# Sums of squares for the second block's query and key norms: two fp32r passes over parts made on GpSimd, two steps later, in place of one fp32 product

## The chip, the cores and the metric

The kernel runs on one core of one Trainium2 chip. The metric is the device time of one execution in microseconds, lower is better. The engines are called as the profile calls them: PE is TensorE, with PEld for its weight loads; ACT is ScalarE; DVE is VectorE; POOL is GpSimd; SP only issues transfers.

## What is computed

Two transformer blocks on 512 tokens of width 1024. The change lies in the second block, where the queries and keys of eight heads (those of the chunked attention with relative positions) are normalised by their root mean square over the 64 numbers of a head:

```
def rmsnorm_2(x, g):
    xf = x.astype(jnp.float32)
    y = xf * lax.rsqrt(jnp.mean(xf * xf, axis=-1, keepdims=True) + EPS)
    return (y * g.astype(jnp.float32)).astype(x.dtype)
...
        q_ca = rmsnorm_2(hs(q_ca, N_CA_HEADS), g_q[l])
        k_ca = rmsnorm_2(hs(k_ca, N_CA_HEADS), g_k[l])
        o_ca = chunked_relpos_attention(q_ca, k_ca, hs(v_ca, N_CA_HEADS), rel_bias[l])
```

## The kernel before

Large products are made from two parts of each operand: an upper part rounded to fp32r and a lower part, the rest. One product of 128x128 by 128x512 is then three fp32r matmuls (upper by upper, upper by lower, lower by upper), lines L2247 to L2249. ACT makes the upper part of each weight (L726), DVE subtracts it to get the lower part (L1306).

The stretch that the change touches is the loop over `steps_s` = 188 steps. It stands once in the program of each engine, and the order on an engine is the order in which the code was written. A step is three matmuls on PE, one eighth of a projection of 128 columns by 512 tokens. Steps 0 to 63 are eight such projections: for each pair of heads p = 0 to 3 the queries (`sub` 0) and the keys (`sub` 1), into PSUM banks 0 and 1. Steps 64 to 95 make the values of the other attention, and so on. Between steps stand "beats": scores (L2394), transposes (L2416) and value products (L2440, L2445) of the attention of heads whose queries and keys are ready. `PACE_S` says how many beats follow each step; none with work in it stands before step 33.

Each of the eight projections ends at a step n = 8m + 7, and is normalised by this chain (`SQUARES` lists the eight steps):

1. ACT squares the projection out of its bank into `sq` (L1128), at step n.
2. PE multiplies `sq` by `blk`, a matrix with ones in two 64x64 blocks, which sums the squares of a head and spreads the sum over its rows (L2678). This is one fp32 product of 128x128 by 128x512, after step n + 2 (`LAG_SUM`). I call it the sum product.
3. ACT takes Ln of the sum and Exp of -0.5 times that (L1098, L1100), at step n + 3 (`LAG_ROOT`).
4. DVE multiplies the bank by the result and by the gain into `qk` (L1780), at step n + 4 (`LAG_NORM`), and counts `qn` up by one. The bank is free then.

PE waits for `qn` before it writes a bank again. For the first seven projections that is at step n + 9 (step 16 waits for the first, and so on). For the last one, which ends at step 63, it is step 68, the first of the second block of values: four steps after step 64, because the values are made in groups of four steps.

POOL has little to do in this stretch. In the order of its program it issues the loads of the last of 48 tiles of the modulation weights (L2157; DVE's L1315 consumes them, and a load waits until the tile that had its place is consumed), then writes a masked corner into each of the eight bias tables once the table has arrived (L2180), with one small memset between the second and third (L2185).

## Time and profile before

| | us |
|---|---|
| median of 3 runs | 957.02 (956.65 to 957.07) |
| the profiled execution, its own time | 957.26 |
| its span, first to last instruction | 955.5 |
| PE busy | 943.3 (99%) |
| DVE busy | 690.3 (72%) |
| ACT busy | 563.2 (59%) |
| POOL busy | 93.7 (10%) |

Between the span and the execution's own time lie 1.8 us in which no instruction is recorded. The granted TensorE clock is full in every slice. In the timeline a matmul's duration overlaps with the next one's: what a matmul occupies of PE is the distance between starts. The fp32 sum product is recorded as two matmuls (x2).

### The profile page before, as it was taken

How to read it: one execution, taken by the hardware profiler on the slowest of the kernel's cores; microseconds unless marked ns; L12 is line 12 of the kernel's file. 1: busy time of each engine (PE TensorE's matmuls, PEld its weight loads, DVE VectorE, ACT ScalarE, POOL GpSimd, SP SyncE). 2: the span in 40 equal slices, each digit the busy share in tenths (PEclk: the TensorE clock that was granted, in tenths of full speed). 3: DMA queues.
4: the chain of work that ended last, by engine and by line, in shares of the span. 5: the costliest groups of instructions: out<-in, count | busy, mean ns of one | idle time of the engine just before them, and what ended most of it. 6: DMA issues, size and time to landing. Idle time of an engine off the chain costs nothing.

```text
span 955.5 us, 13280 instructions
## 1 busy us (share of the span) xinstructions
PE 943.3 (99%) x4728; PEld 787.9 (82%) x4728; DVE 690.3 (72%) x1270; ACT 563.2 (59%) x1107; POOL 93.7 (10%) x182
## 2 busy tenths in 40 slices
PE   8999999999999999999999999999999999999998
PEld 7878988878888887877788777898888888888887
DVE  6487888878788766667768896857544853673988
ACT  6448787753233257479987664556745634644562
POOL 4001101011122102100000000110000000000110
PEclk9999999999999999999999999999999999999999
DMA  8205222149788653833442423465877567486773
GB/s 305 86 24 190 68 79 88 50 158 348 279 316 281 201 134 127 310 111 98 128 173 72 127 67 122 142 175 136 204 215 177 164 195 194 119 233 193 171 186 110
DMA packets 34899, 156.57 MB, mean 164 GB/s; under 512 B 5242, under 2 KB 5498, under 8 KB 22163
## 3 DMA queue, kind: packets, MB, share of 16 engines
q1 hardware_dynamic: 21042, 103.51, 31.2%
q0 software_dynamic: 11152, 49.29, 21.0%
q10 hardware_dynamic: 2640, 2.93, 0.9%
q8 instruction: 38, 0.62, 0.3%
q14 instruction: 27, 0.21, 0.1%
HBM read 144.61 MB, written 5.27 MB: 157 GB/s over the span
## 4 chain that ended last, share of the span: by engine, by line
PE 85%; DVE 8%; ACT 3%; DMA 2%; issue 1%; ACTq 0%; POOL 0%; DVEq 0%; POOLq 0%
PE psum L2247 25%; PE psum L2248 25%; PE psum L2249 25%; PE psum L2416 3%; PE psum L2394 2%; PE psum L2445 1%; DMA raw<-in_wall 1%; PE psum L2440 1%; DVE wl L1306 1%; DVE p_sb L1506 1%; PE psum L2678 1%; DVE hl L1345 1%; DMA v_ca<-v_ca 1%; DVE ptl L1518 1%; DVE xt L1341 1%
## 5 line engine op out<-in xcount | busy, mean ns | idle before, releaser
L2247 PE MATMUL psum<-hh,wh 128*128 128x512 f32 (+2 forms) x736 | 277.7, 377 | 0.7 <-DVE hl L1345 0.6
L2249 PE MATMUL psum<-hh,wl 128*128 128x512 f32 (+2 forms) x736 | 270.1, 367 | 0.0
L2248 PE MATMUL psum<-hl,wh 128*128 128x512 f32 (+2 forms) x736 | 270.1, 367 | 0.0
L1306 DVE TENSOR_TENSOR wl<-raw,wh 128x512 fp32r<-128x512 f32 x336 | 218.8, 685 | 38.3 <-ACT wh L726 37.7
L726 ACT ACTIVATE wh<-raw 128x512 fp32r<-128x512 f32 x336 | 193.2, 621 | 70.3 <-PE psum L2249 64.0
L2247 PEld LDWEIGHTS psum<-hh,wh 128*128 128x128 f32 x736 | 138.4, 188 | 24.5 <-DVE hl L1345 1.6
L2249 PEld LDWEIGHTS psum<-hh,wl 128*128 128x128 f32 x736 | 138.3, 188 | 23.2
L2248 PEld LDWEIGHTS psum<-hl,wh 128*128 128x128 f32 x736 | 138.6, 188 | 20.4 <-issue 1.2
L2247 PE MATMUL psum<-wh,ah 128*128 128x512 f32 x192 | 76.1, 396 | 0.4 <-ACT p_sb L872 0.4
L2249 PE MATMUL psum<-wh,al 128*128 128x512 f32 x192 | 74.9, 390 | 0.0
L2248 PE MATMUL psum<-wl,ah 128*128 128x512 f32 x192 | 74.8, 389 | 0.0
L2416 PE MATMUL psum<-ident,p_sb 128*128 128x128 f32 (+1 forms) x272 | 46.4, 274 | 2.3 <-DVE ptl L1518 1.7
L1209 ACT ACTIVATE two<-psum 128x512 f32<-128x512 f32 x32 | 19.1, 597 | 49.0 <-PE psum L2249 48.9
L2247 PEld LDWEIGHTS psum<-wh,ah 128*128 128x128 f32 x192 | 36.1, 188 | 8.7 <-issue 1.0
L2416 PEld LDWEIGHTS psum<-ident,p_sb 128*128 128x128 f32 (+1 forms) x272 | 32.6, 135 | 12.3 <-issue 4.1
L860 ACT ACTIVATE p_sb<-p_sb,sm 128x528 f32<-128x528 f32 (+3 forms) x64 | 36.2, 565 | 11.1 <-DVE sm L1492 10.9
L2249 PEld LDWEIGHTS psum<-wh,al 128*128 128x128 f32 x192 | 36.0, 188 | 7.7
L2205 POOL DMA_DIRECT2D raw<-in_wall x20 | 17.4, 868 | 251.8 <-DMA raw<-in_wall 141.7
L2248 PEld LDWEIGHTS psum<-wl,ah 128*128 128x128 f32 x192 | 36.1, 188 | 6.7
L866 ACT ACTIVATE p_sb<-p_sb,sm 128x528 f32<-128x528 f32 (+3 forms) x64 | 35.8, 560 | 0.4 <-DVE sm L1497 0.2
L889 ACT ACTIVATE pth<-psum 128x128 fp32r<-128x128 f32 (+4 forms) x72 | 32.2, 447 | 5.9 <-PE psum L2416 5.3
L2249 PE MATMUL psum<-wh,s_y 128*128 128x512 f32 (+1 forms) x92 | 34.9, 380 | 0.0
(367 smaller groups left out, 1729.6 us busy)
## 6 DMA issues: line engine op xcount, KB each, us to landing
raw<-in_wall SPq DMA_DIRECT2D x79, 1024.0 KB, 5.5
raw<-in_wall POOLq DMA_DIRECT2D x20, 1024.0 KB, 8.0
wa<-in_wada POOLq DMA_DIRECT2D x24, 512.0 KB, 6.0
gt<-in_wada POOLq DMA_DIRECT2D x20, 512.0 KB, 6.9
xt<-in_xcols SPq DMA_DIRECT2D x8, 264.0 KB, 7.8
cb<-c_rows SPq DMA_DIRECT2D x8, 264.0 KB, 3.4
x<-in_x SPq DMA_DIRECT2D x4, 512.0 KB, 10.2
x_kept<-x SPq DMA_DIRECT2D x4, 512.0 KB, 2.9
```

Source lines behind the costliest of these rows:

```text
L726: e.activation(parts_at(w, c)[0], raw_of(w, c), ACT.Copy).then_inc(a["wh"], 1)
L860: e.activation(block_p(h, i), block_p(h, i), ACT.Exp, bias=nmx, scale=1.0 if h in FG else -1.0, accum_out=su).then_inc(a["exp"], 1)
L866: e.activation(block_p(h, i), block_p(h, i), ACT.Copy, scale=mx).then_inc(a["norm"], 1)
L889: e.activation(ph[0:rows, PT[j]:PT[j] + w_], bank[bk][0:rows, 0:w_], ACT.Copy).then_inc(a["turn"], 1)
L1209: e.activation(two[:, n % 2, :], bank[w1_bank(n)], ACT.Relu).then_inc(a["r"], 1)
L1306: e.tensor_tensor(lower_, raw_of(w, c), upper_.bitcast(F32), ALU.subtract).then_inc(v["wl"], 1)
L2205: e.dma_start(raw_at(i), wall[W_MLP + 8 * q + 4 + m], accum_op=ALU.add).then_inc(d[f"wa{i}"], 16)
L2247: e.matmul(out_, lh, rh, start=start, stop=False, skip_group_check=True)
L2248: e.matmul(out_, lh, rl, start=False, stop=False, skip_group_check=True)
L2249: return e.matmul(out_, ll, rh, start=False, stop=stop, skip_group_check=True)
L2394: ins = e.matmul(dst[:, size * j:size * j + size], q[:, 128 * i:128 * i + 128], k[:, size * j:size * j + size], start=k is k_up, stop=k is ...
L2416: ins = e.transpose(bank[bk][0:keys, 128 * (i - i0):128 * (i - i0) + 128], head(h)[0][:, o:o + keys], ident[:, :])
```

## The change

The sum product becomes two fp32r matmuls. `sq` is split first, on POOL: a copy rounded to fp32r, then the difference between `sq` and the copy, both into a new buffer `sq_parts`. PE multiplies each part by `blk` and adds them up in the bank. `blk` gets the type fp32r. The three lags grow by two: the sum product stands after step n + 4, Ln and Exp at n + 5, the multiplication at n + 6. There is one buffer for the parts, so POOL waits for the sum product before (`ss`). POOL's remaining masks are woven into its new loop over the steps. A semaphore of POOL, `rs1`, is renamed `norm`, and counts the new instructions as well.

```diff
-        blk = sb("blk", [128, 128])
+        blk = sb("blk", [128, 128], F32R)
...
+        parts_q = sb("sq_parts", [128, 2, SEQ], F32R, where=bq)
...
-        LAG_SUM, LAG_ROOT, LAG_NORM = 2, 3, 4
+        LAG_SUM, LAG_ROOT, LAG_NORM = 4, 5, 6
...
             e.wait_ge(v["m"], 24)
-            for h in CA:
+            def table_mask(h):
                 e.wait_ge(d[f"bt{h % 2}"], 16 * (h // 2 - 3))
                 e.memset(bt[h % 2][0:64, 448:512], NEG).then_inc(g["bt"], 1)
-                if h == 9:
+
+            def square_parts(p, sub):
+                n = 2 * p + sub
+                e.wait_ge(a["sq"], n + 1)
+                if n:
+                    e.wait_ge(t["ss"], n)
+                e.tensor_copy(sq_parts[0], sq[:, sub, :]).then_inc(g["norm"], 1)
+                e.wait_ge(g["norm"], 12 + 2 * n + 1)
+                e.tensor_tensor(sq_parts[1], sq[:, sub, :], sq_parts[0].bitcast(F32), ALU.subtract).then_inc(g["norm"], 1)
+
+            table_mask(8)
+            table_mask(9)
+            for n in range(steps_s):
+                if n in SQUARES:
+                    square_parts(*SQUARES[n])
+                if n == 31:
                     for j in range(4):
                         e.wait_ge(d[f"x{4 + j}"], 32)
                     e.wait_ge(v["tile"], 48)
                     e.memset(dv[0][0:1, :], 0.0).then_inc(g["strip"], 1)
+                for b_ in range(first_s[n - 15], first_s[n + 1]) if n % 16 == 15 else ():
+                    if beats_s[b_] and beats_s[b_][0] == "S" and beats_s[b_][2] == 0 and beats_s[b_][1] + 2 in CA:
+                        table_mask(beats_s[b_][1] + 2)
...
                 if n - LAG_SUM in SQUARES:
                     p, sub = SQUARES[n - LAG_SUM]
-                    e.wait_ge(a["sq"], 2 * p + sub + 1)
+                    e.wait_ge(g["norm"], 12 + 4 * p + 2 * sub + 2)
                     if p or sub:
                         e.wait_ge(a["ln"], 2 * p + sub)
                     else:
                         e.wait_ge(v["vca"], 3)
-                    e.matmul(bank[2], blk[:, :], sq[:, sub, :], start=True, stop=True).then_inc(t["ss"], 1)
+                    e.matmul(bank[2], blk[:, :], sq_parts[0], start=True, stop=False)
+                    e.matmul(bank[2], blk[:, :], sq_parts[1], start=False, stop=True).then_inc(t["ss"], 1)
```

POOL's program at the start of the stretch, before: the last tile loads (the destination `x` is a part of `x1`), then the masks of the bias tables in `sgt`.

```order
L2157 DMA x<-in_wada 128x1024 [waits dve_tile] x2
L2180 MEMSET sgt 64x64 [waits dma_bt0,dve_m]
L2180 MEMSET sgt 64x64 [waits dma_bt1]
L2185 MEMSET x 1x512 [waits dma_x7,dma_x6,dve_tile,dma_x5,dma_x4]
L2180 MEMSET sgt 64x64 [waits dma_bt0]
```

The same place after:

```order
L2162 DMA x<-in_wada 128x1024 [waits dve_tile] x2
L2185 MEMSET sgt 64x64 [waits dma_bt0,dve_m]
L2185 MEMSET sgt 64x64 [waits dma_bt1]
L2192 CAST sq_parts<-two 128x512 [waits act_sq]
L2194 TENSOR_TENSOR sq_parts<-two,sq_parts 128x512 [waits pool_norm]
L2192 CAST sq_parts<-two 128x512 [waits pe_ss,act_sq]
L2194 TENSOR_TENSOR sq_parts<-two,sq_parts 128x512 [waits pool_norm]
```

The first split stands behind the last tile load and two masks.

PE's program from the end of step 65 to the end of step 67, before (`two` is the buffer that `sq` names):

```order
L2249 MATMUL psum<-wh,hl 128x512
L2678 MATMUL psum<-two,blk 128x512 [waits act_ln,act_sq]
L2416 MATMUL psum<-ident,p_sb 128x128 [waits dve_turn,act_norm]
L2416 MATMUL psum<-ident,p_sb 128x128 x3
L2247 MATMUL psum<-wh,hh 128x512 [waits dve_wl]
L2248 MATMUL psum<-wl,hh 128x512
L2249 MATMUL psum<-wh,hl 128x512
L2394 MATMUL psum<-ah 128x128 [waits dve_score]
L2394 MATMUL psum<-al,ah 128x128
L2247 MATMUL psum<-wh,hh 128x512 [waits dve_wl]
L2248 MATMUL psum<-wl,hh 128x512
L2249 MATMUL psum<-wh,hl 128x512
```

The same stretch after, from the transposes behind step 65 on:

```order
L2439 MATMUL psum<-ident,p_sb 128x128 x3
L2270 MATMUL psum<-wh,hh 128x512 [waits dve_wl]
L2271 MATMUL psum<-wl,hh 128x512
L2272 MATMUL psum<-wh,hl 128x512
L2417 MATMUL psum<-ah 128x128 [waits dve_score]
L2417 MATMUL psum<-al,ah 128x128
L2270 MATMUL psum<-wh,hh 128x512 [waits dve_wl]
L2271 MATMUL psum<-wl,hh 128x512
L2272 MATMUL psum<-wh,hl 128x512
L2701 MATMUL psum<-sq_parts,blk 128x512 [waits act_ln,pool_norm]
L2702 MATMUL psum<-sq_parts,blk 128x512
L2270 MATMUL psum<-wh,hh 128x512 [waits dve_qn]
```

The last sum product has moved behind steps 66 and 67, directly ahead of the matmul of step 68 that waits for `qn`.

## Rows read from the trace of the kernel before

**Rows 1.** The page, busy time by engine: us, share of the span, instructions.

```profile
PE 943.3 (99%) x4728; PEld 787.9 (82%) x4728; DVE 690.3 (72%) x1270; ACT 563.2 (59%) x1107; POOL 93.7 (10%) x182
```

**Rows 2.** Windows: stretch, its us, busy PE, PEld, DVE, ACT, POOL, PEclk, DMA.

```profile
424.00:462.00 38.00, 37.71 (x188) 29.43 (x187) 28.91 (x82) 36.84 (x87) 0.44 (x3) 1.00 0.39 123
```

**Rows 3.** Timeline of PE around the first sum product: start, us, line, operands.

```profile
399.87 0.39 PE L2247 MATMUL psum<-hh,wh 128*128 128x512 f32 x1
...
401.00 0.39 PE L2249 MATMUL psum<-hh,wl 128*128 128x512 f32 x1
401.23 1.02 PE L2678 MATMUL psum<-two,blk 128*128 128x512 f32 x2
...
402.32 0.40 PE L2248 MATMUL psum<-hl,wh 128*128 128x512 f32 x1
```

**Rows 4.** The chain that ended last, four of its sum products: start, us, what.

```profile
401.39 0.86 PE psum L2678 x2
...
407.74 0.86 PE psum L2678 x2
...
428.91 0.86 PE psum L2678 x2
...
438.33 0.86 PE psum L2678 x2
```

**Rows 5.** Timeline of ACT in the first normalisation: the square, then Ln.

```profile
400.07 0.60 ACT L1128 ACTIVATE two<-psum 128x512 f32<-128x512 f32 x1 [1.85 <-PE psum L2249]
402.29 0.69 ACT L1098 ACTIVATE two<-psum,eps 128x512 f32<-128x512 f32 x1 [1.62 <-PE psum L2678]
```

**Rows 6.** Timeline of DVE there: a tile, its end, the multiplication.

```profile
400.94 1.22 DVE L1315 CUSTOM_DVE_ANT_0 mis<-x,mis 128x1024 f32<-128x1024 f32 x1
402.08 0.08 DVE L1315 DVE_READ_ACCUMULATOR2_ANT sm<- 128x1 f32 x1
403.67 0.75 DVE L1780 SCALAR_TENSOR_TENSOR qk<-psum,prm,two 128x512 f32<-128x512 f32 x1 [1.51 <-ACT two L1100]
```

**Rows 7.** Timeline of POOL there: the last tile load, two masks.

```profile
402.66 0.54 POOL L2157 DMA_DIRECT2D x<-in_wada  x1 [1.30 <-DVE sm L1315]
403.19 0.26 POOL L2180 MEMSET sgt<- 64x64 f32 x2
```

**Rows 8.** Timeline of POOL early in the program: copies of 16 columns to fp32r.

```profile
7.11 0.20 POOL L2102 CAST hm<-hh 128x16 fp32r<-128x16 f32 x1 [1.11 <-DVE hl L1336]
...
13.23 0.66 POOL L2103 CAST hm<-hl 128x16 fp32r<-128x16 f32 x1
```

**Rows 9.** Timeline of DVE in the same stretch as rows 8.

```profile
7.33 0.69 DVE L1306 TENSOR_TENSOR wl<-raw,wh 128x512 fp32r<-128x512 f32 x1 [0.29 <-ACT wh L726]
...
13.15 0.69 DVE L1306 TENSOR_TENSOR wl<-raw,wh 128x512 fp32r<-128x512 f32 x1
```

**Rows 10.** Groups of POOL by form: busy, mean ns of one, idle before.

```profile
L2173 POOL TENSOR_TENSOR sm<-sm,half 128x2 f32<-128x2 f32 x4 | 2.9, 726 | 0.3
...
L2115 POOL MEMSET pth<- 128x512 f32 x1 | 0.5, 531 | 0.1
...
L2074 POOL MEMSET ones<- 128x128 f32 x1 | 0.2, 205 | 0.3 <-POOLq L2849 0.3
```

**Rows 11.** Timeline of PE: last sum product, end of step 67, step 68.

```profile
456.94 1.02 PE L2678 MATMUL psum<-two,blk 128*128 128x512 f32 x2
...
459.61 0.39 PE L2249 MATMUL psum<-wh,hl 128*128 128x512 f32 x1
460.28 0.50 PE L2247 MATMUL psum<-wh,hh 128*128 128x512 f32 x1 [0.29 <-DVE qk L1780]
```

**Rows 12.** Timeline of ACT there: Ln, then attention work and a weight's upper part.

```profile
458.08 0.70 ACT L1098 ACTIVATE two<-psum,eps 128x512 f32<-128x512 f32 x1
...
459.35 0.71 ACT L866 ACTIVATE p_sb<-p_sb,sm 128x512 f32<-128x512 f32 x1
...
460.44 0.62 ACT L726 ACTIVATE wh<-raw 128x512 fp32r<-128x512 f32 x1
```

More of the change, by code:

```diff
@@ L205, in program @@
         br.close()
+        bq = ExitStack()
+        sb("under_q", [128, 3072], where=bq)
+        parts_q = sb("sq_parts", [128, 2, SEQ], F32R, where=bq)
+        bq.close()
         gt = sb("gt", [128, 2, D])
@@ L277, in program @@
         sq = two
+        sq_parts = [parts_q[:, i, :] for i in range(2)]
         v_rows = (rows[:, 3072:3584], rows[:, 3840:4352], v_end[:, 0:512], rows[:, 1024:1536])
@@ L333, in program @@
                  "s", "sl", "x3", "score", "max", "rcp", "scan_s", "dv", "turn", "o", "oz", "ol")
-        g = sems("pool_", "const", "hm", "rs0", "rs1", "rs3", "mask", "bt", "strip")
+        g = sems("pool_", "const", "hm", "rs0", "norm", "rs3", "mask", "bt", "strip")
         def home(w):
@@ L1022, in keep @@
             def keep(i):
-                e.wait_ge(g["rs1"], 3 * i + 3)
+                e.wait_ge(g["norm"], 3 * i + 3)
                 e.activation(x1[:, i, :], scaled[:, i % 2, :], ACT.Copy, scale=sm[:, 128 + 2 * i:129 + 2 * i]).then_inc(a["xk"], 1)
@@ L1696, in norms @@
             def norms(i):
-                e.wait_ge(g["rs1"], 3 * i + 3)
+                e.wait_ge(g["norm"], 3 * i + 3)
                 e.wait_ge(t["tp"], i) if i else e.wait_ge(v["ol"], 4)
@@ L2081, in _ @@
                             pattern=[[-1, 128]], channel_multiplier=1).then_inc(g["const"], 1)
-            e.memset(blk[:, :], 0.0).then_inc(g["const"], 1)
+            e.memset(blk[:, :].bitcast(F32), 0.0).then_inc(g["const"], 1)
             e.wait_ge(g["const"], 6)
-            e.memset(blk[0:64, 0:64], 1.0).then_inc(g["const"], 1)
-            e.memset(blk[64:128, 64:128], 1.0).then_inc(g["const"], 1)
+            e.memset(blk[0:64, 0:64].bitcast(F32), 1.0).then_inc(g["const"], 1)
+            e.memset(blk[64:128, 64:128].bitcast(F32), 1.0).then_inc(g["const"], 1)
             e.wait_ge(g["const"], 8)
@@ L2167, in _ @@
                 e.wait_ge(a["nsq"], 2 * i + 1)
-                e.tensor_scalar(r[:, 0:1], m1, EPS, None, ALU.add).then_inc(g["rs1"], 1)
+                e.tensor_scalar(r[:, 0:1], m1, EPS, None, ALU.add).then_inc(g["norm"], 1)
                 e.wait_ge(a["nsq"], 2 * i + 2)
-                e.wait_ge(g["rs1"], 3 * i + 1)
-                e.tensor_scalar(r[:, 1:2], r[:, 0:1], EPS, m2, ALU.mult, ALU.add).then_inc(g["rs1"], 1)
-                e.wait_ge(g["rs1"], 3 * i + 2)
-                e.tensor_tensor(r, r, half[:, 0:2], ALU.pow).then_inc(g["rs1"], 1)
+                e.wait_ge(g["norm"], 3 * i + 1)
+                e.tensor_scalar(r[:, 1:2], r[:, 0:1], EPS, m2, ALU.mult, ALU.add).then_inc(g["norm"], 1)
+                e.wait_ge(g["norm"], 3 * i + 2)
+                e.tensor_tensor(r, r, half[:, 0:2], ALU.pow).then_inc(g["norm"], 1)
             gate(0)
```

## The prediction

> **What bounds the kernel now.** I read the page first: PE is busy 943.3 of 955.5 us [rows 1], so PE's own time counts nearly one for one, and so does any wait it is given. Then the granted clock and the busy time in the stretch of the attention: full clock, PE 37.71 of 38 us, but ACT 36.84 and DVE 28.91 as well [rows 2]. So there are two questions: what PE saves, and which of its waits is new. For the first I read the timeline of PE and the chain [rows 3, 4], for the second ACT, DVE and POOL in the same microseconds [rows 5 to 7], and the end of the eight normalisations, where PE waits already [rows 11, 12]. A difference under 0.2% (1.9 us) could hardly be told from none on this kernel.
>
> **Term 1, the passes: -3.2 us.** The sum product starts at 401.23, and the second matmul of the next step at 402.32; one matmul of that step, 0.23, lies between, so the product occupies 0.86 [rows 3], and the chain gives the same 0.86 [rows 4]. An fp32r matmul of the same shape occupies 401.00 to 401.23, 0.23 [rows 3]. Two take 0.46, so 0.40 is saved, and there are eight: 3.2 us. The weight load hides behind the matmul before it, as for all others. The other side, that fp32r passes with `blk` as weights are slower than those of the projections, I give nothing.
>
> **Term 2, the last sum product: +2.0 us.** Before, two steps of matmuls stand between the last sum product and step 68, and cover most of the way through Ln, Exp and the multiplication: step 67 ends at 459.61 + 0.23 = 459.84, step 68 starts at 460.28, a wait of 0.44 that ends with DVE's `qk` [rows 11]. After, nothing stands between. The way itself is read off the first one: the product ends at 401.23 + 0.86 = 402.09, Ln starts at 402.29, DVE at 403.67 and ends at 404.42 [rows 3, 5, 6], 2.33 us, with PE's start 2.4. ACT would be free just in time: the work that Ln now stands behind ran from 459.35 to 460.44 + 0.52 = 460.96, 1.6 us, and would start at 458.08, where Ln stood [rows 12], so it ends at 459.7; the new product ends at 459.84 - 0.86 + 0.46 = 459.44, and Ln could start 0.2 later. So the wait is 2.4 in place of 0.44: +2.0. Bounds: +1.9 to +2.5, the upper one if ACT is half a microsecond late.
>
> For the other seven the bank is wanted four steps after the product, 4 x 0.68 = 2.7 us (two steps are 399.87 to 401.23 [rows 3]) against 2.4; covered, with 0.3 to spare.
>
> **The price of a split on POOL.** No POOL instruction of this size that reads is in the trace. The copy: 16 columns alone take 0.20 [rows 8]; a memset of 512 columns takes 0.531 and one of 128 takes 0.205 [rows 10], 0.85 ns a column, so 0.20 + 0.42 = 0.62. The subtraction reads two operands: at least the copy's 0.62; at most the 0.73 of the two-column TENSOR_TENSOR [rows 10], which is a power, and two columns' worth of reading, 0.87, so 1.6. I take 0.20 + 512 x 1.7 ns = 1.07, the middle and nearest to a copy with a second read. With 0.1 for each of the two handovers a split takes 1.9 us, 1.45 at least and 2.45 at most.
>
> **Term 3, the first sum product waits for POOL: +3.2 us.** POOL runs in order. Ahead of the first split it must issue the load of the last tile, at 402.66, which waits for DVE's tile that ends at 402.08 + 0.08 = 402.16 [rows 6, 7]; then it writes two masks, from 403.19 to 403.45 [rows 7]. None of that moves. The square is ready at 400.67 [rows 5], so the split starts 2.8 us late. PE comes to the product two steps later than before, at 401.23 + 1.36 = 402.59. Unhindered the split ends at 403.45 + 1.9 = 405.35, a wait of 2.8. But DVE no longer idles at 402.16: the multiplication is now behind another tile of 1.22 and a subtraction of a weight's lower part (0.69 [rows 9], some 0.61 from start to start), which then runs until 404.0. The next paragraph says why POOL has to wait for that: 0.45 more, so 3.2. Bounds: 2.3 with the quickest split, 4.2 with the slowest and another such wait. Everything on PE is queued behind, and nothing behind it makes up for the time, since PE has next to no idle time that it could give back.
>
> **Ports.** A copy of 16 columns on POOL takes 0.20 beside a DVE that starts its subtraction only after it, and 0.66 when it starts 0.08 after a DVE subtraction of two SBUF operands that takes 0.69 [rows 8, 9]: it stands until DVE is done. DVE's instructions in this stretch are often of that kind (tiles of 1.22, lower parts of 0.69), so a split may be held at its start and again between its two halves, and in turn holds up DVE by its 0.6 and 1.1 us. The Trainium skill, "SBUF — State Buffer", section "Who interferes with whom", has a rule for it that speaks against this change: a VectorE instruction with two SBUF inputs contends with a GpSimd instruction that reads SBUF, and whichever comes second blocks until the first has finished. By that rule, the trace agrees where it can (the copy's 0.66), while DVE being held by POOL is in no row.
>
> **Term 4, the other seven splits: +1.8 us.** The first square ends 401.23 - 400.67 = 0.56 before its old product, so with two steps more the split has 0.56 + 1.36 = 1.9 us, where no beats stand between. That holds for the second and third product too (401.39 and 407.74 are 6.35 apart [rows 4], eight bare steps and a product). A free split just fits. One held by a DVE tile between its halves is 1.2 late: I take 0.9 for the second product, which still falls among the last tiles, and 0.5 for the third, among lower parts. Later products are 9.42 apart [rows 4], (9.42 - 0.86)/8 = 1.07 a step, so the split has 2.7 us; 0.4 for all five. Bounds: 0 and 3.5.
>
> **Term 5, ACT and DVE: +0.5 us.** From 424 to 462 ACT is busy 97% of the time [rows 2]. What PE saves at the products there it can't wholly keep, as it runs into ACT's results; and DVE, held by splits, hands lower parts and transposed parts on later. Bounds: 0 and 2.
>
> **Edits at nothing:** the type of `blk` (same memsets), the renamed semaphore, the memset of L2185 behind four splits (its reader on SP comes some 16 steps later), the masks of the bias tables, of which some come a split later; they are wanted by scores several steps on. The cover is gone if a split is held for microseconds, and then a score waits by that much.
>
> **Sum:** -3.2 + 2.0 + 3.2 + 1.8 + 0.5 = +4.3 us. The profiled execution took 957.26, 0.24 over the median, and would take 961.6; from the median of 957.02 I forecast 961.3.
>
> **Rivals.**
> - *Quick splits, not slower by what can be told.* If POOL gets its port whenever it asks and a split takes 1.45, the first wait is 2.3 and the others vanish, term 5 too: -3.2 + 2.0 + 2.3 = +1.1, 958.1. For it: the 16-column copies show that a held POOL gets in as soon as DVE is between two instructions. Against: two bare instructions of 512 columns with handovers hardly fit. It decides where a split takes under 1.9 us. Chance 0.16, of which most is within 0.2%.
> - *Faster: the first wait is not there.* One mechanism could give it: DVE consumes the tile that POOL's last load waits for earlier, as nothing ahead of it depends on PE, and POOL is free when the square is ready. Then -3.2 + 2.0 = -1.2 with fitting splits, 955.8. It decides where the first wait is under 1.2 us; but DVE is packed back to back up to 402.16 with work that doesn't change, so I give it 0.03.
> - *The port costs more: slower still.* Each of the sixteen POOL instructions is held by DVE for half of one of its instructions (0.3 to 0.6), and DVE by POOL; terms 3, 4 and 5 go to 3.8, 3.5 and 1.5: -3.2 + 2.0 + 8.8 = +7.6, 964.6. It decides where splits take over 3 us. Chance 0.24.
> - *The clock falls* during the first wait of some 3 us, the longest on PE in this stretch. No row shows a granted clock below full, nor a wait of this length after PE has started, so nothing is excluded; a few microseconds at half speed would add about 2 us to the forecast, 963.3. Chance 0.07.
> - The forecast's own case, 958.9 to 963: chance 0.50.
>
> **How the numbers follow.** The time is that of the likeliest case. The range must leave out at most 2 in 10: the lower end takes in most of the quick case (958.1 with its spread, cut at 958.0), the upper end goes to 965.5, past the port case's 964.6 but not to the sum of all upper bounds (-3.2 + 2.5 + 4.2 + 3.5 + 2 = +9.0, 966.0). Slower by over 0.2% means above 958.9: 0.50 + 0.24 + 0.07 and a small part of the quick case, 0.83. Faster by over 0.2%, under 955.1: 0.03. The rest, 0.14, is within.
>
> **What would show it.** In the profile of the changed kernel: two sum matmuls start to start 0.23 apart (term 1); PE idle before the first of them, released by POOL's subtraction, some 3 us near 403 to 406 (term 3), then one or two waits under 1.5 us; a wait of 2.4 us at step 68 released by `qk` (term 2); POOL's copy near 0.6 and subtraction near 1.1, longer where DVE runs two SBUF operands (ports), and some of DVE's own subtractions longer than 0.69. I am wrong if the first wait is under 1 us, if POOL's subtraction takes well over 1.6 us, or if waits of the attention (transposed parts, lower parts) grow by more than 2 us in all.

## The result and the profile after

The changed kernel took 966.57 us (median of 5 runs, 965.54 to 968.19), the kernel before 957.02 in the same rounds (956.61 to 957.32). The ratio is 1.0102, with a 95% interval of 1.0091 to 1.0113: slower by 9.5 us, where I had forecast 4.3 and a range that ended at 965.5. The profiled execution of after took 966.59, its span is 964.9 against 955.5 before, so there are 9.4 us to find. The line numbers have moved on: the three projection matmuls are L2270 to L2272 (before L2247 to L2249), the sum matmuls L2701 and L2702, POOL's copy L2192 and subtraction L2194, ACT's square L1133, its Ln L1103 and Exp L1105, DVE's multiplication L1785, its lower parts of weights L1311, of keys L1468, the tiles L1320, a score L2417, the copies on SP L605.

The busy line of the page, which answers to [rows 1]:

```profile
PE 945.0 (98%) x4728; PEld 789.9 (82%) x4728; DVE 694.3 (72%) x1270; ACT 562.9 (58%) x1107; POOL 111.1 (12%) x198
```

PE was to be busy 3.2 us less, and is busy 1.7 us more. Part of these 4.9 us is a matter of the record: around a wait the matmuls show some 0.3 us more of busy time than they occupy among others, and after has five more waits of this kind than before. That is 1.4 us, and the greater part is left, so something also made its matmuls slower. The rest of the 9.4 must be waits. The waits of PE, by what ended them (us in total, times, longest us), three rows of that view:

```profile
PE psum L2701 <- POOL sq_parts L2194: 5.3, 5, 3.0
...
PE psum L2270 <- DVE qk L1785: 2.2, 1, 2.2
...
PE psum L2417 <- issue: 1.6, 1, 1.6
```

PE waits for POOL at five of eight sum products, once for `qk` at step 68, and once 1.6 us ahead of a score for something that the view doesn't name. In the timeline of PE (start, us, line, shapes, in brackets the idle time that the view lists and who ended it) these places are:

```profile
402.25 0.39 PE L2272 MATMUL psum<-hh,wl 128*128 128x512 f32 x1
405.61 0.50 PE L2701 MATMUL psum<-sq_parts,blk 128*128 128x512 f32 x1 [2.97 <-POOL sq_parts L2194]
405.95 0.39 PE L2702 MATMUL psum<-sq_parts,blk 128*128 128x512 f32 x1
...
408.09 0.63 PE L2270 MATMUL psum<-hh,wh 128*128 128x512 f32 x1
408.52 0.63 PE L2271 MATMUL psum<-hl,wh 128*128 128x512 f32 x1
...
414.26 0.50 PE L2701 MATMUL psum<-sq_parts,blk 128*128 128x512 f32 x1 [0.82 <-POOL sq_parts L2194]
...
427.40 0.47 PE L2417 MATMUL psum<-k_sb,q_sb 128*128 128x512 f32 x1 [1.60 <-issue]
...
465.83 0.39 PE L2701 MATMUL psum<-sq_parts,blk 128*128 128x512 f32 x1
466.06 0.40 PE L2702 MATMUL psum<-sq_parts,blk 128*128 128x512 f32 x1
468.68 0.80 PE L2270 MATMUL psum<-wh,hh 128*128 128x512 f32 x1 [2.23 <-DVE qk L1785]
```

Each wait is read from the end of the work before (its start plus 0.23) to the start. A matmul behind a wait starts about 0.1 earlier than it gets going, as its follower comes 0.34 later instead of 0.23; I count that to the wait, which gives 3.2 at the first product. And from 408.09 to 408.52 two starts lie 0.43 apart where 0.23 is usual. The windows (stretch, its us, busy PE, PEld, DVE, ACT, POOL, granted clock, DMA share, GB/s) say why:

```profile
402.00:406.00 4.00, 1.03 (x5) 0.54 (x4) 2.29 (x5) 0.00 (x0) 2.92 (x5) 1.00 0.80 284
...
408.00:410.00 2.00, 2.00 (x6) 1.54 (x6) 2.00 (x4) 0.00 (x0) 0.00 (x0) 0.50 0.00 0
...
466.00:468.00 2.00, 0.46 (x2) 0.02 (x1) 1.41 (x3) 1.97 (x4) 0.00 (x0) 1.00 0.37 147
...
470.00:472.00 2.00, 2.00 (x8) 1.51 (x8) 0.85 (x2) 0.66 (x3) 0.00 (x0) 0.55 0.00 0
```

The granted clock is 0.50, the lower of the two levels (1.2 GHz in place of 2.4), in 408 to 410, after a stretch of 4 us in which PE was busy 1.03. The slow matmuls don't start right behind that wait: up to 406.88 the starts are still 0.23 apart. The clock is low again from 468 to 472 (0.59 and 0.55), behind a stretch of 2 us in which PE was busy 0.46; there the matmuls are slow from the first one behind the wait, at 468.68. In the slices of the page the clock is a 9 everywhere: two stretches of some 3.5 us each don't show in slices of 24 us each.

**The account.** From the starts in the timelines of before and after:

| term | place | predicted | measured |
|---|---|---|---|
| 1 | two passes in place of one fp32 product, eight times | -3.2 | -3.2 |
| 3 | first sum product waits for POOL, 402.48 to 405.7 | +3.2 | +3.2 |
| 4 | 2nd, 3rd, 5th, 7th product wait, about 1.05, 0.7, 1.0, 0.55 | +1.8 | +3.3 |
| 2 | step 68 waits for `qk`, 2.4 against 0.44 | +2.0 | +2.0 |
| 5 | ACT and DVE: small shifts between the fourth product and step 66, none of them a wait of over 0.4 | +0.5 | +0.4 |
| - | first score behind step 33 waits 1.8 against 0.6 | - | +1.2 |
| - | half clock behind the first wait: seven distances of 0.43 and two of 0.36 and 0.29 where 0.23 is usual (1.6), and behind step 68: steps 68 and 69 take 3.32 against 1.90 (1.4) | rival | +3.0 |
| - | a wait for a transfer, far behind: 0.41 against 0.99 | - | -0.6 |
| | sum | +4.3 | +9.3 of 9.4 |

Up to step 69 PE has fallen back by 9.9 us. Then 0.6 of it come back, at a matmul that waits for a transfer of `v_ca`: before it waited 0.99 us, and after it comes later and waits 0.41. The matmul comes 9.3 us later, not 9.9: the transfer has been put off by less than PE, and the wait for it takes up the rest. The two rows, and from the kernel before also the score behind step 33:

```profile
421.75 0.47 PE L2394 MATMUL psum<-k_sb,q_sb 128*128 128x512 f32 x1 [0.46 <-issue]
...
533.56 0.70 PE L2394 MATMUL psum<-v_ca 128*128 128x512 f32 x2 [0.99 <-DMA v_ca<-v_ca]
```

```profile
542.82 0.70 PE L2417 MATMUL psum<-v_ca 128*128 128x512 f32 x2 [0.41 <-DMA v_ca<-v_ca]
```

The rows of POOL for the first two splits, and the same two lines over all eight (duration in ns, least/median/most, then the first and last start):

```profile
402.54 0.54 POOL L2162 DMA_DIRECT2D x<-in_wada  x1 [1.30 <-DVE sm L1320]
403.07 0.26 POOL L2185 MEMSET sgt<- 64x64 f32 x2
403.25 0.64 POOL L2192 CAST sq_parts<-two 128x512 fp32r<-128x512 f32 x1
403.98 1.58 POOL L2194 TENSOR_TENSOR sq_parts<-two,sq_parts 128x512 fp32r<-128x512 f32 x1
...
412.08 2.13 POOL L2194 TENSOR_TENSOR sq_parts<-two,sq_parts 128x512 fp32r<-128x512 f32 x1
```

```profile
L2192 POOL CAST sq_parts<-two x8: 612/619/757, 403.3 to 462.8; 128x512 fp32r<-128x512 f32 x8
...
L2194 POOL TENSOR_TENSOR sq_parts<-two,sq_parts x8: 1263/1652/2128, 404.0 to 463.4; 128x512 fp32r<-128x512 f32 x8
```

The copy takes 0.62, as worked out. The subtraction takes 1.26 when nothing holds it, and 1.65 in the median, above my 1.07 and my upper bound of 1.6. From the start of the copy to the end of the subtraction a split takes 2.0 us when it is free (the fourth and the eighth) and up to 2.8 (the second). My 1.9 counted the two handovers too; counted like that, the free fourth split takes 2.1 from the end of its square. DVE is held as well. The first row is a subtraction that takes 0.68 when it is alone, begun 0.09 after POOL's copy; the second a tiny one of 128x8, 0.17 when alone; the third the lower part of half of a pair's keys, 0.69 for the next half at 423.87, when POOL rests:

```profile
403.34 1.09 DVE L1311 TENSOR_TENSOR wl<-raw,wh 128x512 fp32r<-128x512 f32 x1
...
413.12 1.12 DVE L1325 TENSOR_TENSOR mod<-sm,prm 128x8 f32<-128x8 f32 x1
...
419.77 1.66 DVE L1468 TENSOR_TENSOR low<-qk,k_sb 64x512 fp32r<-64x512 f32 x1
```

Four questions were open after this reading. What do the lags cost without the splits? What do splits cost that nobody waits for? Does the half clock belong to the waits? And what does the score behind step 33 wait for? All times below come with the kernel before measured in the same rounds: 956.85 for experiments 1, 2, 4 and 6, 956.92 for 3, 5, 7 and 8, 957.12 for 9 to 11.

### The profile page after: what moved, and what is told of

Its sections match the earlier page's. It is cut to its first block, busy times and chain, and to the rows that moved or that the text cites. A ratio compares the mean times of both kernels' runs of the same rounds, so it can differ in the third digit from the quotient of the medians.

```text
span 964.9 us, 13303 instructions
## 1 busy us (share of the span) xinstructions
PE 945.0 (98%) x4728; PEld 789.9 (82%) x4728; DVE 694.3 (72%) x1270; ACT 562.9 (58%) x1107; POOL 111.1 (12%) x198
## 4 chain that ended last, share of the span: by engine, by line
PE 81%; DVE 9%; ACT 4%; issue 2%; DMA 2%; POOL 1%; ACTq 0%; DVEq 0%; POOLq 0%
PE psum L2270 24%; PE psum L2271 24%; PE psum L2272 24%; PE psum L2439 2%; PE psum L2417 2%; PE psum L2468 1%; DMA raw<-in_wall 1%; PE psum L2463 1%; DVE wl L1311 1%; DVE p_sb L1511 1%; POOL sq_parts L2194 1%; DVE hl L1350 1%; ACT p_sb L865 1%; DVE ptl L1523 1%; DVE xt L1346 1%
## 5 line engine op out<-in xcount | busy, mean ns | idle before, releaser
L2270 PE MATMUL psum<-hh,wh 128*128 128x512 f32 (+2 forms) x736 | 277.1, 377 | 0.7 <-DVE hl L1350 0.6
L2272 PE MATMUL psum<-hh,wl 128*128 128x512 f32 (+2 forms) x736 | 270.6, 368 | 0.0
L1311 DVE TENSOR_TENSOR wl<-raw,wh 128x512 fp32r<-128x512 f32 x336 | 220.1, 689 | 38.5 <-ACT wh L731 37.9
L2270 PEld LDWEIGHTS psum<-hh,wh 128*128 128x128 f32 x736 | 138.9, 189 | 23.8 <-DVE hl L1350 1.4
L2272 PEld LDWEIGHTS psum<-hh,wl 128*128 128x128 f32 x736 | 138.8, 189 | 23.4
L2270 PE MATMUL psum<-wh,ah 128*128 128x512 f32 x192 | 76.0, 396 | 0.4 <-ACT p_sb L877 0.4
L2272 PE MATMUL psum<-wh,al 128*128 128x512 f32 x192 | 74.9, 390 | 0.0
L2270 PEld LDWEIGHTS psum<-wh,ah 128*128 128x128 f32 x192 | 36.1, 188 | 8.6 <-issue 1.0
L2272 PEld LDWEIGHTS psum<-wh,al 128*128 128x128 f32 x192 | 36.0, 188 | 7.7
L2272 PE MATMUL psum<-wh,s_y 128*128 128x512 f32 (+1 forms) x92 | 34.9, 380 | 0.0
```

Source lines behind the costliest of these rows:

```text
L1311: e.tensor_tensor(lower_, raw_of(w, c), upper_.bitcast(F32), ALU.subtract).then_inc(v["wl"], 1)
L2270: e.matmul(out_, lh, rh, start=start, stop=False, skip_group_check=True)
L2272: return e.matmul(out_, ll, rh, start=False, stop=stop, skip_group_check=True)
```

## The experiments

### 1. The lags alone

```diff
-        LAG_SUM, LAG_ROOT, LAG_NORM = 2, 3, 4
+        LAG_SUM, LAG_ROOT, LAG_NORM = 4, 5, 6
```

> The kernel before with the three lags of the change (4, 5, 6 in place of 2, 3, 4) and nothing else: the sum product stays fp32, POOL splits nothing. My theory (the added time is made of single waits of PE and of two stretches at half the TensorE clock that follow the two longest of them): the wait at step 68 goes from 0.44 to about 2.4 us (+2.0), the clock is granted at half for about 3 us after it (+1.4), and the first score beat at step 33 waits about 1 us longer, since the keys that it reads are normalised two steps later (+0.8). Together +4.2 us, 961.2. Rival (the clock fell in the changed kernel for other reasons, not because of the wait): +2.8 us, 959.8, with the clock full all the way. Second rival (the lags cost nothing, all of it is POOL): 957.0.

Measured: 960.76 (960.43 to 961.71), ratio 1.0042 [1.0027, 1.0057], so +3.9 us for nothing in return. The timeline of PE:

```profile
422.21 0.47 PE L2394 MATMUL psum<-k_sb,q_sb 128*128 128x512 f32 x1 [1.65 <-issue]
...
464.19 0.50 PE L2247 MATMUL psum<-wh,hh 128*128 128x512 f32 x1 [2.23 <-DVE qk L1780]
```

Step 68 waits 2.4, as in after and as predicted, and 2.0 of the 3.9 are found. But the clock stayed full behind it (1.00 in every window from 462 to 470), so a wait of this length doesn't always bring it down. My theory had 1.4 us for the clock, and these did not come in the profiled execution; that the sum (961.2) came out near is no support for them. At step 33 the score waits 1.65 in place of 0.46, +1.2; experiments 9 to 11 are about that. The profiled execution is 3.2 us longer than that of the kernel before (960.47 against 957.26), and 2.0 and 1.2 are just that, since small shifts (+0.6) and the wait for `v_ca` (0.34 in place of 0.99) cancel. What the median has beyond that is not placed.

### 2. Splits that nobody waits for

POOL splits rows of `hh` into a buffer that nobody reads, each when its square is done. Lags and sum product are those of the kernel before; POOL's masks stand in its loop as in the changed kernel. The first two lines stand in place of the split's own, against the changed kernel's POOL program:

```diff
+                e.wait_ge(g["norm"], 12 + 2 * n)
+                e.tensor_copy(sq_parts[0], hh[:, n, META:TOK].bitcast(F32)).then_inc(g["norm"], 1)
...
+                e.tensor_tensor(sq_parts[1], hh[:, n, META:TOK].bitcast(F32), sq_parts[0].bitcast(F32), ALU.subtract).then_inc(g["norm"], 1)
```

> The kernel before, lags 2, 3, 4 and fp32 sum product, but POOL does a copy and a subtraction of the size of the split at each of the eight places, on data that lies still (a part of the normalised input), into a buffer that nobody reads. No engine waits for it. It prices what POOL's reading costs DVE alone. My theory (the waits of PE for the split are the price, contention on the port is small): +0.3 to +1.5 us, 957.8; DVE instructions that are held by a subtraction on POOL show durations up to 1.3 us longer than their 0.69. Rival (contention between POOL and DVE is the main cause of the 9.5 us): +3 us or more, above 960.

Measured: 957.90, ratio 1.0013 [1.0003, 1.0022]: +1.0 us. POOL's first two splits here:

```profile
403.67 0.62 POOL L2191 CAST sq_parts<-hh 128x512 fp32r<-128x512 f32 x1
404.38 1.30 POOL L2193 TENSOR_TENSOR sq_parts<-hh,sq_parts 128x512 fp32r<-128x512 f32 x1
407.38 1.60 POOL L2191 CAST sq_parts<-hh 128x512 fp32r<-128x512 f32 x1 [1.69 <-ACT two L1133]
```

DVE's tile ahead of the third of these:

```profile
407.30 1.21 DVE L1320 CUSTOM_DVE_ANT_0 mis<-wa,mis 128x1024 f32<-128x1024 f32 x1
```

The same copy takes 0.62 or 1.60; the 1.60 start 0.08 behind that tile, and end some 0.5 behind its end. DVE's busy time in 412 to 424 rises from 7.62 to 9.62 us at the same number of instructions (14). PE pays for it in one place, the score behind step 33, 1.36 in place of 0.46. So each engine holds the other, yet the price without anyone waiting for POOL is only 1 us: the contention by itself isn't what makes the change slow.

### 3. Splits with the old lags

```diff
-        LAG_SUM, LAG_ROOT, LAG_NORM = 4, 5, 6
+        LAG_SUM, LAG_ROOT, LAG_NORM = 2, 3, 4
```

> The changed kernel with the three lags of the kernel before (2, 3, 4). My theory (a split on POOL takes 2.0 to 2.9 us from the end of the square, and PE waits for whatever part of it isn't covered): the product comes 0.56 us after the square, so PE waits 4.4 us at the first and 1.4 to 2.3 us at each of the other seven, some 17 us, less the 3.2 us of the passes, with step 68 as before; a stretch at half clock behind the first adds 1.6: +15, 972. Rival (the later lags are what costs, the splits are cheap): below 963.

Measured: 974.71 (972.65 to 975.08), 8.1 us above after. PE's waits, first row:

```profile
PE psum L2701 <- POOL sq_parts L2194: 14.6, 8, 4.0
```

All eight products wait now, 14.6 us against 5.3. On the kernel before the lags cost 3.9 us; with POOL making the parts they gain 8.1 on balance. My theory had one stretch at half clock, and 972. The windows show three, behind the waits of 4.00, 2.17 and 1.83 us ahead of the first three products, and none behind the wait of 2.00 ahead of the fifth:

```profile
416.00:418.00 2.00, 2.00 (x5) 1.60 (x6) 0.00 (x0) 0.93 (x2) 0.00 (x0) 0.54 0.49 205
...
426.00:428.00 2.00, 2.00 (x7) 1.55 (x6) 0.30 (x1) 1.65 (x3) 0.00 (x0) 0.60 0.00 0
...
446.00:448.00 2.00, 2.00 (x12) 1.71 (x12) 2.00 (x7) 2.00 (x6) 0.00 (x0) 1.00 0.00 0
```

### 4. The first split earlier

The first split stands ahead of the last two tile loads and the masks, which had held it until 403.25.

```diff
-            for m in range(40, 48):
+            for m in range(40, 46):
                 load_tile(m)
+            square_parts(0, 0)
+            load_tile(46)
+            load_tile(47)
```

> The changed kernel with one move: POOL's first split stands ahead of the loads of the last two tiles and of the first two masks. My theory: the first wait of PE falls from 3.2 to about 0.6 us (-2.6), and with it goes the stretch at half clock behind it (-1.6): 962.4 against 966.6 for the changed kernel. Rival (the clock falls there whatever PE waits): -2.6 alone, 964.0, with a stretch at half clock still near 407.

Measured: 963.49 (962.37 to 964.16), 3.1 under after, 1.1 above my 962.4 and 0.5 under the rival's 964.0; what decides between the two is the clock below. The wait for the first product is 1.00 in place of 2.97, and the one for the second 1.19 in place of 0.82. Both splits run beside DVE's tiles and both subtractions take 2.12; the first of them, and the product that waits for it:

```profile
401.18 2.12 POOL L2188 TENSOR_TENSOR sq_parts<-two,sq_parts 128x512 fp32r<-128x512 f32 x1
```

```profile
403.35 0.50 PE L2705 MATMUL psum<-sq_parts,blk 128*128 128x512 f32 x1 [1.00 <-POOL sq_parts L2188]
```

In the windows the granted clock is 1.00 from 402 to 412: the fall behind the first wait has gone with the wait. Behind step 68 it is still there. Of the four executions three had a mean clock of 0.998, and the fourth, with 1.000, was the fastest (962.37).

```profile
406.00:408.00 2.00, 2.00 (x10) 1.66 (x9) 2.00 (x5) 1.16 (x3) 0.49 (x1) 1.00 0.85 344
...
466.00:468.00 2.00, 2.00 (x7) 1.61 (x7) 0.85 (x2) 1.18 (x4) 0.00 (x0) 0.50 0.00 0
```

### 5. The last normalisation as before

To experiment 4 the last of the eight normalisations is put back: one fp32 product, lags 2, 3, 4, no split.

```diff
+        SUM_AT = {m_ + (2 if m_ == 63 else 4): x_ for m_, x_ in SQUARES.items()}
...
+                    if n > 63:
+                        e.matmul(bank[2], blk[:, :].bitcast(F32), sq[:, sub, :], start=True, stop=True).then_inc(t["ss"], 1)
```

> As early_split, with the last of the eight normalisations as in the kernel before: fp32 product of the squares, lags 2, 3, 4. My theory: the wait at step 68 falls from 2.4 to 0.4 us (-2.0), the fp32 product gives back 0.4, and the stretch at half clock that early_split shows behind step 68 goes (-1.4): 963.5 - 3.0 = 960.5. Rival (the clock falls in that stretch whatever precedes it): 961.9, with the clock below full from 462 to 470.

Measured: 960.72 (960.67 to 961.58), ratio 1.0038 [1.0023, 1.0053]; 2.8 under experiment 4. The wait at step 68 is gone and the clock is full there. Two microseconds are the wait, 0.4 goes the other way since the fp32 product is back, and the remaining 1.2 agree with the half clock. The window that answers to the last one above:

```profile
466.00:468.00 2.00, 2.00 (x11) 1.59 (x10) 0.85 (x2) 1.98 (x7) 0.00 (x0) 1.00 0.00 0
```

### 6. One pass, without POOL

If the aim is to spare the fp32 product, there is a shorter way: ACT writes the squares rounded to fp32r, and PE makes one fp32r matmul (`blk` is fp32r as in the change). The lower part of the squares is left out of the sum, so this kernel and those of experiments 7, 8, 10 and 11 compute a coarser sum than the two compared above. Lags as before.

```diff
-                    e.activation(sq[:, sub, :], bank[sub], ACT.Square).then_inc(a["sq"], 1)
+                    e.activation(sq_r[:, sub, :], bank[sub], ACT.Square).then_inc(a["sq"], 1)
...
-                    e.matmul(bank[2], blk[:, :], sq[:, sub, :], start=True, stop=True).then_inc(t["ss"], 1)
+                    e.matmul(bank[2], blk[:, :], sq_r[:, sub, :], start=True, stop=True).then_inc(t["ss"], 1)
```

> The kernel before, lags 2, 3, 4, but ACT writes the squares rounded to fp32r, and the sum product is one fp32r matmul of them: no lower part, no POOL. It leaves the lower part of the squares out, so the sums are a little coarser than those of the kernel before. It prices the passes alone. If a pass occupies 0.23 as in the changed kernel's profile, each sum product falls from 0.86 to 0.23, 8 x 0.63 = 5.0 us: 952.0. Rival (ACT, busy 97% from 424 to 462, gives the time back in the attention): -2 to -3.5, 953.5 to 955.

Measured: 954.28 (953.82 to 955.03), ratio 0.9974 [0.9964, 0.9984]: faster than both, by 2.6 of the 5.0 us (8 x 0.63) that PE saves. Where the rest went:

```profile
420.38 0.47 PE L2398 MATMUL psum<-k_sb,q_sb 128*128 128x512 f32 x1 [1.14 <-issue]
...
457.98 0.50 PE L2251 MATMUL psum<-wh,hh 128*128 128x512 f32 x1 [0.88 <-DVE qk L1784]
```

Both waits grew, from 0.46 and 0.29 (by the same view), 1.3 us of the 2.4 that are missing. Most of the rest are waits for DVE's transposed and lower parts (lines L1525 and L1310 there), in all 1.1 us longer than before: PE comes earlier to results that don't. That is my term 5, with DVE and SP in place of ACT.

### 7. One pass with late lags

```diff
-        LAG_SUM, LAG_ROOT, LAG_NORM = 2, 3, 4
+        LAG_SUM, LAG_ROOT, LAG_NORM = 4, 5, 6
```

> As one_pass (one fp32r matmul of rounded squares, no POOL; the lower part of the squares is left out), with the lags of the change (4, 5, 6). If the price of the lags (3.9 us measured on the kernel before) is the same here, 954.3 + 3.9 = 958.2. The 8.4 us that are then left to the changed kernel are the second pass (8 x 0.23 = 1.8), PE's waits for POOL (6.4 by its trace) and the clock. Rival (the gain of the passes was held back by the same waits that the lags lengthen, so the two don't add): 959.5 to 961, as lag_only.

Measured: 958.50 (957.06 to 959.34), 4.2 above experiment 6, where the lags alone had cost 3.9. The two edits add up within the spread. Of its ten executions five had a mean granted clock of 0.998 and took 958.85 to 959.34; of the others three had 0.999 (957.44 to 958.14) and two 1.000 (957.06 and 957.61). By their medians the two halves are 1.5 us apart, which fits a stretch at half clock that comes or doesn't. The profiled one had it, behind a wait of 2.4 us at step 68:

```profile
462.00:464.00 2.00, 2.00 (x8) 1.57 (x7) 0.85 (x2) 0.76 (x3) 0.00 (x0) 0.58 0.00 0
```

### 8. One pass with early lags

```diff
-        LAG_SUM, LAG_ROOT, LAG_NORM = 2, 3, 4
+        LAG_SUM, LAG_ROOT, LAG_NORM = 1, 2, 3
```

> As one_pass, with the lags 1, 2, 3, so the whole normalisation comes a step (0.68 us) earlier (the lower part of the squares is left out). In one_pass PE waits 1.14 us at the score beat of step 33, for the copied keys, and 0.88 at step 68; both chains start with the sum product, so both waits should fall by up to 0.68: -1.3. The product then stands 0.12 us behind the end of the square less than it needs, 0.1 to 0.3 us at each of eight: +1.2. So about 954.2, within 1 us of one_pass. Rival (the waits at steps 33 and 68 hang on something else): 955.5.

Measured: 955.37 (954.51 to 956.00), ratio 0.9982 [0.9973, 0.9992], by the medians 1.1 slower than experiment 6, though the intervals overlap and the two profiled executions took the same 955.03. The time is that of my rival (955.5), its reason is not: the wait at step 33 fell from 1.14 to 0.26, and the one for `qk` at step 68 is gone from the view. What took it back stands at the products: each of the first four comes about 0.27 later than a step earlier would give, for the square isn't done, and the sixth waits 0.79 for its square (released by ACT, at 435.50). Earlier is not simply better.

### 9. What the score behind step 33 waits for

The view says "issue", so no engine. The keys of a pair are copied to the other 64 rows by transfers on SP's queue, and the last of them is what I compared with the score. After, SP's last issue of them (start, us from issue to landing):

```profile
424.24 1.24 SPq L605 DMA_DIRECT2D low<-low  x2
```

| kernel | `low` issued | landed | score starts | between the last two | wait |
|---|---|---|---|---|---|
| before | 418.56 | 419.80 | 421.75 | 1.95 | 0.46 |
| after | 424.24 | 425.48 | 427.40 | 1.92 | 1.60 |
| lags alone | 419.02 | 420.26 | 422.21 | 1.95 | 1.65 |
| splits that nobody waits for | 419.22 | 421.00 | 422.95 | 1.95 | 1.36 |
| one pass | 417.19 | 418.42 | 420.38 | 1.96 | 1.14 |
| one pass, lags 1, 2, 3 | 416.75 | 417.99 | 419.93 | 1.94 | 0.26 |

The score starts 1.92 to 1.96 us behind the landing, whether the transfer takes 1.24 or 1.78, and so it does in the four other kernels that wait there (experiments 4, 5, 7 and 11): that names the transfer. What fills these 1.9 us no view shows. In turn it waits for DVE's lower part of the keys' second half, made at step 29, and with the lags at 4, 5, 6 the third projection's Ln and Exp stand ahead of the upper part on ACT (step 28) and its multiplication ahead of the lower part on DVE (step 29). They belong to queries of another pair and have nothing to do with these keys. So for that projection alone the order is turned round:

```diff
-                if n - LAG_ROOT in SQUARES:
+                if n - LAG_ROOT in SQUARES and n != 28:
                     inverse(*SQUARES[n - LAG_ROOT])
...
                         keys(p, qk[:, p % 2, 1, :], (part,))
+                if n == 28:
+                    inverse(*SQUARES[n - LAG_ROOT])
```

On DVE likewise, the multiplication behind `keys` at n = 29.

> The kernel before with the three lags at 4, 5 and 6 (as in lag_only), and one thing turned round for the third projection: on ACT its Ln and Exp stand behind the second half of the first keys instead of ahead of it (step 28), on DVE its multiplication stands behind the lower part of the same half (step 29). In lag_only PE stood 1.65 us ahead of the first score of step 33, and the copies of the keys' lower part on SP's queue, issued at 419.02, were 3.19 us ahead of that score. Theory: those copies are what the score waits for, and they are late because the keys' second half stands behind Ln, Exp and the multiplication of a projection that has nothing to do with it. ACT idled 1.15 us ahead of that Ln, so the half and its lower part then come some 2 us sooner and the wait is gone: 960.76 - 1.65 = 959.1. Rival: the score waits for something else, the time stays at 960.8; or the multiplication now comes too late for the bank at step 32, 960 and a wait there that ends with qk. The wait at step 68 stays at 2.2 either way.

Measured: 958.91 (957.91 to 960.69), ratio 1.0022 [1.0013, 1.0031], 1.9 under the lags alone. The lower part is done 2.8 us earlier, the copies go 2.9 us earlier, and PE doesn't wait there:

```profile
415.84 0.69 DVE L1465 TENSOR_TENSOR low<-qk,k_sb 64x512 fp32r<-64x512 f32 x1
...
417.49 0.75 DVE L1782 SCALAR_TENSOR_TENSOR qk<-psum,prm,two 128x512 f32<-128x512 f32 x1 [0.95 <-ACT two L1100]
```

```profile
416.14 1.23 SPq L600 DMA_DIRECT2D low<-low  x2
```

```profile
420.03 0.39 PE L2400 MATMUL psum<-k_sb,q_sb 128*128 128x512 f32 x1
```

The clock shows again in the spread: three of the ten executions had 0.998 and took 960.13 to 960.69, seven had 1.000 and took 957.91 to 959.66, 1.5 us less by their medians. The profiled one was of the seven, so where the clock fell in the three isn't recorded; the wait at step 68 (2.2 us) is the longest of the stretch.

### 10. The same turn in the one-pass kernel

Ln, Exp and multiplication of the third projection at steps 28 and 29, behind the keys; everything else as in experiment 6.

```diff
-        LAG_SUM, LAG_ROOT, LAG_NORM = 2, 3, 4
+        LAG_SUM = 2
+        ROOT_AT = {m_ + (5 if m_ == 23 else 3): x_ for m_, x_ in SQUARES.items()}
+        NORM_AT = {m_ + (6 if m_ == 23 else 4): x_ for m_, x_ in SQUARES.items()}
```

> one_pass (954.3 us) with the same turn: Ln and Exp of the third projection stand at step 28 behind the second half of the first keys in place of step 26, the multiplication at step 29 behind the lower part. All lags else are those of the kernel before. Theory: the wait of 1.14 us ahead of the score of step 33 goes, and the multiplication still ends just before step 32 wants the bank: 953.2. Rival: the bank is late by up to half a microsecond and half of the gain is left, 953.8; or the wait belongs to something else, 954.3 or more.

Measured: 952.49 (952.40 to 953.35), ratio 0.9955 [0.9941, 0.9968], the fastest here: 4.6 us under before, and 1.8 under experiment 6, where the wait to be removed was 1.14; the other 0.7 I haven't placed. The score doesn't wait, with the copies issued 2.1 us sooner than in experiment 6, and the multiplication is still in time for step 32:

```profile
415.12 1.23 SPq L606 DMA_DIRECT2D low<-low  x2
```

```profile
418.60 0.39 PE L2406 MATMUL psum<-k_sb,q_sb 128*128 128x512 f32 x1
```

### 11. Another way to the same keys

The lags 1, 2, 3 for the third projection alone, 2, 3, 4 elsewhere.

```diff
+        SUM_AT = {m_ + (1 if m_ == 23 else 2): x_ for m_, x_ in SQUARES.items()}
```

> one_pass (954.3 us) with the lags 1, 2 and 3 for the third projection alone, 2, 3 and 4 for the others. With 1, 2, 3 everywhere the wait ahead of step 33 had fallen from 1.14 to 0.26, and a new one of 0.79 had come at 435.5, where ACT was late with a square. Theory: the first is kept and the second doesn't come: 954.3 - 0.9 = 953.4. Rival: the sum product of the third projection waits for its square by what the score gains, 954.3.

Measured: 953.67 (953.27 to 953.99), ratio 0.9966 [0.9953, 0.9978]; 0.6 under experiment 6 by the medians (the intervals overlap), with the wait at 0.53 in place of 1.14, and without the late square of experiment 8. It gains less than the turn: Ln and Exp still stand ahead of the keys' second half on ACT.

## Why the prediction was wrong

**The direction and half of the sum were right.** Term 1: the sum matmuls start 0.23 apart (465.83 and 466.06), -3.2. Term 2: the chain through Ln, Exp and multiplication takes 2.4 when nothing stands between product and reader; +2.0, in after and again in experiment 1. Term 3: the wait for the first split came out at 3.2 to the tenth, but partly by two errors that cancel. The split began at 403.25, not at 403.45 + 0.45, because the second mask's 0.26 overlaps with the copy and DVE didn't hold the copy; and the subtraction took 1.58 instead of 1.07, since it was the subtraction that had to wait for DVE. That the number came out to the tenth is luck.

**The clock was the largest miss, +3.0 us.** I had it as a rival at 0.07, with a price of 2 us in one place. What failed is the step "nothing is excluded" followed by a small chance: my own forecast had two gaps on PE, of 3.2 and of 2.4 us, in a stretch with hardly any idle time, and for each I should have asked what the clock does behind it. The runs tell the two apart. Behind a first wait of 3.0 the clock fell (1.6 us); with that wait cut to 1.0 it stayed full. Behind the wait of 2.2 to 2.4 at step 68 it fell in the profiled executions of after and of experiments 4 and 7, but not in those of experiments 1 and 9; without the wait (experiment 5) it stayed full. In experiment 3 it fell behind waits of 4.00, 2.17 and 1.83, and not behind one of 2.00. So the length of the wait alone doesn't decide. What does is open: I didn't try it. The Trainium skill, "TensorE: Matmul & The Clock Gate", section "HAM oscillation — how this bites in real kernels", says that a wait inside a kernel can bring the clock down, so that the work behind it starts slow. By that rule, the runs agree that the clock falls behind waits, at step 68 in part of the executions only. The work behind the wait starts slow at step 68, but not behind the first wait, where the starts stayed 0.23 apart for the next 0.9 us before they went to 0.43.

**Term 4 was mis-sized, 3.3 in place of 1.8.** Two steps failed. The first is the price of the subtraction: "0.20 + 512 x 1.7 ns = 1.07", a second operand at the price of the first. A free one takes 1.26, so a split takes 2.1 us from the end of the square, and what I called a split that just fits was 0.2 too long before anything held it. Beside DVE's instructions of two SBUF operands the subtraction took 1.7 to 2.1, in all four cases of this term in which PE waited; the median of all eight is 1.65. By my own sign of being wrong, "well over 1.6", that is at the border. The second is the time that a split has. "(9.42 - 0.86)/8 = 1.07 a step, so the split has 2.7 us" spreads the beats evenly over the steps, but they don't lie evenly. At the fifth product the square ended at 434.85 + 0.57 = 435.42 and the work ahead of the product at 436.88 + 0.23 = 437.11, 1.7 us:

```profile
434.85 0.57 ACT L1133 ACTIVATE two<-psum 128x512 f32<-128x512 f32 x1
```

```profile
436.88 0.40 PE L2272 MATMUL psum<-hh,wl 128*128 128x512 f32 x1
438.01 0.50 PE L2701 MATMUL psum<-sq_parts,blk 128*128 128x512 f32 x1 [0.73 <-POOL sq_parts L2194]
```

At the seventh it was 2.1. So these two waited 1.55 together, where I had 0.4 for all five later products; the second and third waited 1.75 where I had 1.4. The ports did what [rows 8, 9] had shown for the small copies, in both directions (0.62 to 1.60 for a copy on POOL, 0.68 to 1.09 for a subtraction on DVE), at 1.0 us in all where nobody waits for POOL (experiment 2). The rival of the dear port, with splits of over 3 us, didn't come: the longest took 2.8.

**A chain was missed, +1.2 us.** I followed the results of the moved steps only to PE's bank: "for the other seven the bank is wanted four steps after the product, covered". That was true, none of them waited. But Ln, Exp and the multiplication moved past other work on their own engines too, and stood ahead of the keys' second half on ACT and on DVE. From there it went over SP's transfer to the first score. Experiments 9 and 10 show it by turning that order round alone, on the late lags and on one pass; in the changed kernel itself I didn't turn it. The row was in the trace of before, an idle time of 0.46 ahead of that score, the longest between the first product and step 68, and I had not asked what it waited for.

**Term 5** was about right in size, 0.4 for 0.5, but its rows are small shifts that I haven't traced to ACT or DVE one by one. What I left out is the opposite: a wait that was there before, for a transfer, takes up 0.6 us when PE is put off by more than the transfer. Where PE really came earlier (experiment 6) waits gave back 2.4 of 5.0 us, and the turn of experiment 10 gained 1.8.

**The parts that were run** are the lags, +3.9, of which the turned order takes back 1.9, and splits that nobody waits for, +1.0. They don't simply add to the 9.5, as both lengthen the same wait behind step 33; the account above, from one execution each, is the sum. With the first split earlier (experiment 4) and the last normalisation as before (experiment 5) the scheme still stands at 960.7, above the kernel before. With these lags a saving of 0.40 a product doesn't pay for a split of 2 to 2.8 us. Still later lags, or the turned order with the splits, were not run.

## What to carry to other kernels

When a step is moved later, look not only at who reads its result, but at what it now stands in front of on its own engines, and follow that to the next transfer. Price every new gap on TensorE twice: once for itself and once for the clock behind it, as 3 us of waiting cost 4.6 here. Price the room that a moved step gets from the instructions that really stand there, not from the mean step. And before a product is split to use a cheaper type, ask whether the engine that writes the operand can write the cheaper type at once: that needed no new instruction, and with one order turned round it gave 952.5 where the split gave 966.6. It is not the same sum, as the lower part is left out, so it is a choice only where the coarser sum will do.

## What the runs showed of the hardware

- POOL's subtraction of two fp32 tiles of 128x512 into fp32r takes 1.26 us unhindered, its copy to fp32r 0.61.
- POOL and DVE hold each other, small instructions too: beside POOL's subtraction a DVE subtraction of 128x8 took 1.12 us in place of 0.17, and behind a DVE tile a POOL copy took 1.60 in place of 0.62.
- Waits of 1.8 us and more on PE in an otherwise busy stretch (1.83, 2.17, 2.23, 2.35, 2.97 and 4.00 us) were followed by some 3 us at half clock, at 1.4 to 1.6 us a time where it was read off. Others of 2.00 and 2.23 us were not, and waits of up to 1.66 us were not in any window read.
- A matmul that waited for a transfer within SBUF started 1.92 to 1.96 us behind the landing that the view gives, in ten kernels.
